# Three pads that set where the streamed and the stationary operands of the projections begin in SBUF

## The reference

```python
def first_block(x, mem, ...):
    h = layer_norm(ALPHA*h + 0.5 * (silu(h @ w_gate) * (h @ w_up)) @ w_down)      # 1024 -> 2816 -> 1024
    h = layer_norm(ALPHA*h + token_mixers(h, w_in, ...) @ w_out)                  # w_in: 1024 -> 3072
    h = layer_norm(ALPHA*h + cross_attention(h, layer_norm(mem), wq, wk, wv, wo)) # mem: 256 tokens
    h = layer_norm(ALPHA*h + 0.5 * swiglu(h, ...))                                # second FFN
def second_block(x, c, ctx, ...):
    z  = modulate(x)  @ w_in          # 1024 -> 8704: q, k, v, convolution branches, gates
    zc = modulate(ctx) @ w_in[:, k and v]                                         # ctx: 256 tokens
    ya, yb, yc = neighbourhood_attention(z, zc), short_conv(z), conformer(z)
    x = x + gate * (ga*(ya @ w_a) + gb*(yb @ w_b) + gc*(yc @ w_c)) @ w_o
```

## The kernel before, in words

| buffers | role | before | after |
|---|---|---|---|
| `w_hi`, `w_lo` | stationary; moving in token strips | 128 | 128 |
| `a_hi`, `a_lo`, `hid_*`, `m_*`, `y_*`, `mix_h`, `mix_l` | moving; `a_*` stationary in token strips | 128 | 320 |
| `side_hi`, `side_lo` (memory) | moving; stationary in token strips and in the attention's values | 128 | 320 |
| `memv_hi`, `memv_lo` | stationary in the attention's values | 128 | 320 |
| `xpt_hi`, `xpt_lo` (turned probabilities) | moving in the attention's values | 128 | 0 |
| `ctx_hi`, `ctx_lo` (context, for `ctxk` alone) | moving | 320 | 320 |

## Time and profile before

### The profile page before, as it was taken

How to read it: one execution, slowest core, us unless ns; L and a number is a source line. 1 busy time by engine, 2 the same in 40 slices (tenths; PEclk the granted TensorE clock), 3 DMA queues, 4 the chain that set the end, 5 groups by cost and what they waited for, 6 DMA issues and landing times.

```text
span 1706.6 us, 22901 instructions
## 1 busy us (share of the span) xinstructions
PE 1691.5 (99%) x8500; PEld 1394.7 (82%) x8500; DVE 994.7 (58%) x1341; ACT 683.6 (40%) x975; POOL 166.8 (10%) x158
## 2 busy tenths in 40 slices
PE   9999999999999999999999999999999999999999
PEld 7888888888787888888888888877778787788887
DVE  5333339987965784666333333457976869844442
ACT  4222232246454465434222223346454445732330
POOL 0000000112004521013000000013011020000000
DMA  5333247633122353223332233323333222243331
GB/s 216 98 98 98 91 138 231 222 121 119 52 98 66 109 182 137 67 82 123 98 98 94 92 130 117 109 87 118 85 99 95 86 83 86 74 123 109 104 109 62
DMA packets 51476, 188.05 MB, mean 110 GB/s; under 512 B 5776, under 2 KB 6288, under 8 KB 50512
## 3 DMA queue, kind: packets, MB, share of 16 engines
q1 hardware_dynamic: 44640, 161.50, 29.7%
q10 hardware_dynamic: 5184, 16.00, 2.9%
q0 software_dynamic: 1584, 9.60, 1.6%
HBM read 182.89 MB, written 4.19 MB: 110 GB/s over the span
## 4 chain that ended last, share of the span: by engine, by line
PE 89%; DVE 7%; ACT 2%; issue 1%; DMA 0%; POOL 0%; SPq 0%; DVEq 0%; ACTq 0%; POOLq 0%
PE proj L422 83%; DVE w_lo L414 1%; PE aux L1859 1%; PE aux L1846 1%; PE aux L1619 1%; PE aux L1836 1%; DVE y L2016 0%; ACT w_hi L407 0%; DVE score L1221 0%; DVE qk L1264 0%; DVE md L1242 0%; PE aux L566 0%; DVE qk L1265 0%; PE aux L1839 0%; DVE md L1241 0%
## 5 line engine op out<-in xcount | busy, mean ns | idle before, releaser
L414 DVE TENSOR_TENSOR w_lo<-raw,w_hi 128x1024 fp32r<-128x1024 f32 x300 | 380.5, 1270 | 388.8 <-ACT w_hi L407 382.0
L422 PE MATMUL proj<-a_hi,w_hi 128*128 128x512 f32 (+1 forms) x1536 | 600.8, 391 | 3.3 <-DVE a_lo L909 1.8
L422 PE MATMUL proj<-a_hi,w_lo 128*128 128x512 f32 (+1 forms) x1536 | 591.3, 385 | 0.0
L422 PE MATMUL proj<-a_lo,w_hi 128*128 128x512 f32 (+1 forms) x1536 | 591.0, 385 | 0.0
L407 ACT ACTIVATE w_hi<-raw 128x1024 fp32r<-128x1024 f32 x300 | 315.3, 1053 | 233.4 <-PE proj L422 164.3
L422 PEld LDWEIGHTS proj<-a_hi,w_hi 128*128 128x128 f32 x1536 | 288.5, 188 | 67.9 <-issue 5.8
L422 PEld LDWEIGHTS proj<-a_lo,w_hi 128*128 128x128 f32 x1536 | 288.7, 188 | 58.4 <-issue 2.9
L422 PEld LDWEIGHTS proj<-a_hi,w_lo 128*128 128x128 f32 x1536 | 288.5, 188 | 58.5
L422 PE MATMUL proj<-hid_hi,w_hi 128*128 128x512 f32 (+1 forms) x374 | 142.6, 381 | 0.0
L422 PE MATMUL proj<-hid_hi,w_lo 128*128 128x512 f32 (+1 forms) x374 | 140.9, 377 | 0.0
L422 PE MATMUL proj<-hid_lo,w_hi 128*128 128x512 f32 (+1 forms) x374 | 140.8, 377 | 0.0
(11 more groups left out here) (368 smaller groups left out, 2011.1 us busy)
## 6 DMA issues: line engine op xcount, KB each, us to landing
raw<-stream SPq DMA_DIRECT2D x303, 512.0 KB, 3.5
ctxk<-ada_in ACTq DMA_DIRECT2D x12, 512.0 KB, 3.7
ctxv<-ada_in ACTq DMA_DIRECT2D x12, 512.0 KB, 3.9
out<-h ACTq DMA_DIRECT2D x7, 256.0 KB, 2.0
h<-x_in SPq DMA_DIRECT2D x3, 512.0 KB, 8.7
btab<-rpb_in POOLq DMA_DIRECT2D x4, 384.0 KB, 3.5
cond_row<-cond_in ACTq DMA_DIRECT2D x1, 1024.0 KB, 5.9
side<-mem_in POOLq DMA_DIRECT2D x1, 1024.0 KB, 5.2
```

What stands on the lines that cost most here:

```text
L414: nc.vector.tensor_tensor(w_lo[:, st.slot], raw[:, st.slot], w_hi[:, st.slot].bitcast(F32), ALU.subtract).then_inc(lo_ready, 1)
L422: mm = nc.tensor.matmul(dst, a, b, start=start and n == 0, stop=stop and n == 2)
```

## The change

Three unused tiles are allocated. The first, 48 words (192 bytes) long, stands behind the weight buffers and moves all that follows by 192 bytes. The second, also 192 bytes, stands ahead of `xp`, `xpt_hi` and `xpt_lo`. The third, of (-48 - 48) mod 128 = 32 words (128 bytes), stands ahead of `ctx_hi` and `ctx_lo` and leaves these at 320 modulo 512. No instruction is added, taken away or moved on any engine.

```diff
+OFF_WORDS = 48
...
         w_lo = sb("w_lo", [P, RING, SB * P], F32R)
+        sb("weights_offset", [P, OFF_WORDS])
         h = sb("h", [P, KD, T])
...
             memv_hi, memv_lo = (sb(n, [P, MB, W5], F32R, ph) for n in ("memv_hi", "memv_lo"))
+            sb("turned_offset", [P, OFF_WORDS], F32, ph)
             xp = sb("xp", [P, 2, 2, M], F32, ph)
             xpt_hi, xpt_lo = (sb(n, [P, 2, MB, M], F32R, ph) for n in ("xpt_hi", "xpt_lo"))
             xs = sb("xs", [P, 3, 8, 2], F32, ph)
+            sb("ctx_offset", [P, (-OFF_WORDS - 48) % P], F32, ph)
             ctx_hi = sb("ctx_hi", [P, KD, M], F32R, ph)
```

## The result

The changed kernel takes 1743.51 us (median of 4 runs, 1742.62 to 1744.54), the kernel before 1708.52 us beside it. The ratio is 1.0206, 95% interval 1.0194 to 1.0219: slower by 35 us, where 41 us less had been forecast. The profiled execution has a span of 1742.4 us, 35.8 more than before. Line 422 is line 426 now; the program is else the same on every engine.

A forecast was written before the change was run, and what follows sets the result against it. TensorE's matmul spacing was taken as the bound: 47.0 us gained on projections, less losses where other engines set the pace and 0.75 us in the loop, gave 41.7 us, hence 1667 us; range for 8 in 10, 1660 to 1684.

The forecast's parts named there:

- What bounds the kernel: Whole kernel: matmuls fill 99% of the span, so it is as long as its matmuls are spaced.
- reading the context's keys as an experiment that the kernel had made: Keys of the context, 192 bytes past the weights: 113.3 ns spacing, against 120.0 ns for the memory's keys at 0 bytes.
- a moving operand and the next weight load do disturb each other: 256-column keys of memory and context: the disturbance was claimed to cost 6.7 ns or more per matmul.
- The rule that was set against rows 6 and 7: Two independent read ports on TensorE; by it the change would do nothing, 1708.4 us; rows 6 and 7 time 256-column keys.
- The step that failed: 7050 projection matmuls, any width: each comes 6.67 ns sooner, 47.0 us in all; 512 columns every 220 ns.
- The bounds: 512-column projections: from above, all 13.7 ns of excess could go; from below, no gain or a loss of 6.7 ns.
- The rival "slower": Every 512-column matmul takes 6.7 ns more, 6390 of them, +43 us, 1751 us; chance 0.05.
- the third and fourth pass over a block's 512 bytes: 512-column streams could meet the load there, 192 bytes on; 256-column streams pass only twice; price 6.7 ns per matmul.
- Token strips: 336 matmuls whose weights move, 320 bytes past the block: 2.2 us of the 47.0, 0 to 6.7 ns each possible.
- The losses: Gain taken off where another engine sets the pace (0.5, 1.2, 1.45, 0.5, 0.25, 0.65 us) and in the neighbourhood loop (0.75 us).
- The stretch from 1174 us: 1174 to 1201 us, another engine setting the pace: 101 matmuls, whose 0.65 us gain was counted as lost.
- What would show it: Timeline: 220 ns starts at 100 us, memory's keys at 113.3 ns, context's keys unchanged, TensorE idle time up 4 to 8 us.

The follow-up runs named there:

- all192: The kernel before with all buffers, the weights too, beginning 192 bytes later and every relative distance kept; 1708.41 us.

## Why the prediction was wrong

- *What bounds the kernel* was right: TensorE's spacing. A difference of 6.3 ns became 36 us almost without loss.
- *That the distance between moving and stationary operand counts, and not alignment*, was right, shown by `all192`. So was reading the context's keys as an experiment that the kernel had made: at 256 bytes of distance they lost their advantage (119.9 ns). At 256 columns the memory's keys went to 113.4 ns, as forecast, but for the first part of them alone; the rest went to 117.8. The context's keys were to stay at 113.3 and went to 117.7. So even where the step was seen it was worth less: 3.6 ns on the mean, 2.3 us for all the narrow streams, where 660 x 6.67 ns = 4.4 us had been counted. That "a moving operand and the next weight load do disturb each other" names one of two candidates; the runs do not tell the next block from the block in use.
- *The rule that was set against rows 6 and 7.* The Trainium skill, "TensorE: Matmul & The Clock Gate", section "Step-by-step: what each phase is for", says that TensorE reads the streamed operand and the weights through a read port each. What the prediction drew from it, that no address could matter, does not agree with the runs: 226.7 to 233.3 ns with the distance, while a shift of all buffers together changes nothing.
- *The step that failed:* "The excess before is the same at both widths (13.7 and 13.3 ns), so it is paid once per matmul. I take the 256-column difference, 120.0 - 113.3 = 6.7 ns, for both." The first sentence holds at distance 0. It says nothing about distance 192, where all I had was one width. There the excess is 6.7 (or 11), 13.3 and 20 ns at 256, 384 and 512 columns. The term of the sum, a gain of 7050 x 6.67 ns = 47.0 us, had the wrong sign: the 6054 wide matmuls lose up to 6.67 ns each, at most 40 us (37.5 us in the table above), and the narrow ones gain 2.3 us. That the spacing at 512 columns got worse is shown; why the excess grows with the width stays open.
- *The bounds* had named the right end, "the wide stream could gain nothing or lose the same 6.7 ns". The range of the forecast did not include it, though no row told gain, nothing and loss apart at 512 columns. The rival "slower", at 0.05, gave the right spacing (226.7 + 6.7 ns), the right place and 1751 us. It missed by 7.5 us, as it left out the narrow streams' gain, charged the token strips the whole step, and let no stretch hide any of it. Its number was in part luck: it took over the 256-column step with the other sign, where by the table of widths the loss of 16 cycles is the sum of a gain of 16 and of 32 more for the columns from 256 to 512. Its place, the third and fourth pass over a block's 512 bytes, agrees with that table (16 cycles more at 384 columns, 32 at 512) but was not put to a test of its own.
- *Token strips:* 320 bytes turned out as 64 modulo 256, at 229.3 ns in the mixer but 233.3 in the memory's values: a loss of 0.7 us, where a gain of 0 to 2.2 us had been left open. Of the mixer's 192 token matmuls only some 175 lie in the stretch from 418 to 478 us, as rows 9 say.
- *The losses* (4.55 us in stretches that another engine sets, 0.75 us in the loop) were priced for a gain. For a loss, four of the stretches show that they indeed keep their length. Between the same two matmuls, TensorE takes 14.14 and 14.11 us (362 to 376 us, before and after), 60.09 and 60.12 (418 to 478), 42.20 and 42.15 (566 to 608), 26.01 and 25.91 (686 to 712). In the mixer 0.4 us of slower token matmuls are hidden so. The stretch from 1174 us is longer by 0.27 us, where its 101 wide matmuls make 0.64. So these readings were sound, and small beside the term that failed.
- *What would show it:* the text had set "above 227 ns" as the point from which the slower case decides, and the timeline showed 233. Of the other signs, the loads of 188 ns in the memory's keys came. The duration of `proj<-a_hi,w_hi` went to 394 ns by its median, not from 389 to 382 or 383, and TensorE's idle time fell to 14.4 us where it was to grow by 4 to 8.

## What to carry to other kernels

A spacing that is a few ns above streaming, over thousands of matmuls, is worth a look at where the operands begin. But an effect that was seen at one width must be measured at the width that carries the time, before it is multiplied by the count. Where a sum is one small number times 7000, its sign is the prediction, and a bound from both sides has to be in the range.

## What the runs showed of the hardware

- The spacing of fp32r matmuls, each with its own weight load, depends on the distance between the moving operand and the stationary blocks, modulo 256 bytes: 226.7 ns at 0 and 256, 229.1 at 64, 232.9 at 128, and 233.2 to 233.5 at 32, 192 and 224 (512 columns). With all buffers moved together it stays at 226.7.
- At distance 0 the excess over streaming is 32 cycles at 256, 384 and 512 columns. At 192 bytes it is 16 (or 26), 32 and 48. 384 columns were measured in the memory's keys alone.
- The spacing is a rhythm over many matmuls, and one distance can have two: at 192 bytes and 256 columns 113.4 or 117.8 ns, and in token strips at 64 bytes 229.3 or 233.3. Within the three products the starts need not be even: at 192 bytes and 512 columns they are 231 and 236 ns apart in turn. The rhythm was seen to change across a wait.
